# Products with u from PSUM, and all sums of v rows on TensorE, in the last two tiles of an expert layer

## The reference, cut to what matters

```
act = gelu(sum over d of h[t, d] * u[expert(t, head, k), d])
w   = gate(t, head, k) * act
out[t, :] += w * v[expert(t, head, k), :]      over 8 heads and 16 picks
```

## Time and profile before

| | |
|---|---|
| median of 3 runs | 3301.13 us (3296.62 to 3303.43) |
| profiled execution, span from first to last instruction | 3366.8 us |
| granted TensorE clock, mean of the span | 0.927 of full |
| busy share of the span: PE / DVE / POOL / ACT | 79% / 68% / 67% / 22% |
| moved by DMA | 1185.41 MB, mean 352 GB/s |

### The profile page before, as it was taken

The page is one execution under the profiler, slowest core; times in us unless marked ns, Lnnn a source line. Parts: engine busy times, 40 slices in busy tenths (PEclk is TensorE's granted clock), DMA queues, the critical chain, the costliest instruction groups (busy, mean ns, idle before and its releaser), DMA issues.

```text
span 3366.8 us, 25897 instructions
## 1 busy us (share of the span) xinstructions
PE 2658.0 (79%) x7200; PEld 1257.8 (37%) x7200; DVE 2274.4 (68%) x4952; ACT 737.2 (22%) x1644; POOL 2267.3 (67%) x2074
## 2 busy tenths in 40 slices
PE   7866778998888778987887868998888776666667
PEld 3444333444354333433344423334435332222222
DVE  1559964579579984668659994568758995455443
ACT  2411121223221121223221121223322111111111
POOL 0025677777766777777776677777776676777776
PEclk9888899999998899999999889999999898988989
DMA  5248999999999999999999899999999999999998
GB/s 185 75 172 301 345 345 408 406 405 368 361 388 351 379 341 400 407 407 362 350 396 381 325 361 384 405 406 393 358 389 368 335 328 350 346 370 371 368 362 332
DMA packets 351442, 1185.41 MB, mean 352 GB/s; under 512 B 37666, under 2 KB 38212, under 8 KB 351044
## 3 DMA queue, kind: packets, MB, share of 16 engines
q0 software_dynamic: 294912, 1073.87, 84.2%
q1 hardware_dynamic: 56388, 109.88, 8.9%
HBM read 1181.52 MB, written 2.10 MB: 352 GB/s over the span
## 4 chain that ended last, share of the span: by engine, by line
POOL 27%; PE 23%; DVE 20%; issue 17%; DMA 11%; another core or an unknown queue 1%; ACT 1%; DVEq 0%; POOLq 0%; ACTq 0%
POOL v_ring L468 13%; POOL u_ring L468 13%; PE peer_acc L1258 12%; DMA v_ring<-in_peer_v,experts 8%; PE act_bank L1045 5%; DVE u_ring L986 4%; DMA u_ring<-in_peer_u,experts 4%; PE dve_bank L1045 2%; DVE work L752 2%; DVE work L741 1%; DVE work L749 1%; DVE work L738 1%; DVE work L931 1%; DVE work L933 1%
## 5 line engine op out<-in xcount | busy, mean ns | idle before, releaser
L1258 PE MATMUL peer_acc<-v_ring,diag 128*128 128x512 f32 x3584 | 1805.4, 645 | 647.1 <-DMA v_ring<-in_peer_v,experts 296.7
L986 DVE SCALAR_TENSOR_TENSOR u_ring<-u_ring,h 128x1024 f32<-128x1024 f32 x1024 | 1255.2, 1226 | 841.2 <-DMA u_ring<-in_peer_u,experts 730.1
L468 POOL DMA_INDIRECT v_ring<-in_peer_v,experts x1024 | 1146.9, 1120 | 524.3 <-issue 259.6
L468 POOL DMA_INDIRECT u_ring<-in_peer_u,experts x1024 | 1114.9, 1089 | 561.2 <-issue 308.9
L1258 PEld LDWEIGHTS peer_acc<-v_ring,diag 128*128 128x128 f32 x3584 | 688.5, 203 | 1647.7 <-issue 1009.4
L669 ACT ACTIVATE diag<-ident,wts 128x128 f32<-128x128 f32 x896 | 325.8, 397 | 1180.5 <-PE peer_acc L1258 580.9
L1045 PE MATMUL act_bank<-w_ring,hT 128*128 128x512 f32 x768 | 346.4, 598 | 0.7 <-ACT hT L508 0.7
L1045 PEld LDWEIGHTS act_bank<-w_ring,hT 128*128 128x128 f32 x768 | 147.5, 193 | 187.0 <-issue 185.6
L996 DVE SCALAR_TENSOR_TENSOR xs<-v_ring,wts,xs 128x1024 f32<-128x1024 f32 x128 | 164.5, 1285 | 49.5 <-DMA v_ring<-in_peer_v,experts 40.0
L1132 PE MATMUL act_bank<-hT,w_ring 128*128 128x256 f32 x768 | 175.6, 384 | 0.0
L1132 PEld LDWEIGHTS act_bank<-hT,w_ring 128*128 128x128 f32 x768 | 148.6, 194 | 39.4 <-issue 20.9
(11 more groups left out here) (158 smaller groups left out, 1540.0 us busy)
## 6 DMA issues: line engine op xcount, KB each, us to landing
w_ring<-in_w_in SPq DMA_DIRECT2D x24, 2048.0 KB
w_ring<-in_peer_w_q SPq DMA_DIRECT2D x16, 2048.0 KB
w_ring<-in_w_out SPq DMA_DIRECT2D x8, 2048.0 KB
u_ring<-in_peer_u,experts POOLq DMA_INDIRECT x1024
v_ring<-in_peer_v,experts POOLq DMA_INDIRECT x1024
xs<-in_x SPq DMA_DIRECT2D x4, 512.0 KB, 7.2
keysT<-in_peer_sub_keys SPq DMA_DIRECT2D x2, 1024.0 KB
out<-xs SPq DMA_DIRECT2D x4, 512.0 KB
```

Source lines behind the costliest of these rows:

```text
L468: pool.indirect_dma_start(ring[:, n % depth, :], None, table, bass.IndirectOffsetOnAxis(ap=experts[:, tile % TILES, e:e + 1], axis=0),).th ...
L986: tell(nc.vector.scalar_tensor_tensor(out=row, in0=row, scalar=1.0, in1=h2[:, tile % TILES, :], op0=ALU.mult, op1=ALU.mult, accum_out=dots ...
L1258: ins = nc.tensor.matmul(peer_acc[:, j * 512:(j + 1) * 512], diag[:, (v_count(c, s) - 1) % DIAGS, :], v_ring[:, n % V_RING, j * 512:(j + 1 ...
```

## The change

In chunks 48 to 63 (tiles 6 and 7), and only there:

- `slot_u` reads `h` from PSUM. The three `dve_bank` become slices of one PSUM tensor `dve_banks`, and at the first slot of a tile DVE copies `h2` of the tile (128 x 1024) into its first two banks. The multiplication then has one input in SBUF (the u row) and one in PSUM. Its output stays in SBUF.
- `by_vector` is false, so that PE sums all 16 v rows of a chunk and DVE none. ACT makes 16 diagonal matrices per chunk instead of 14.
- The counts of `v_used` follow (`v_count`, `v_done`), and POOL's waits with them.

The number, size and order of the gathers don't change, nor does anything in chunks 0 to 47.

```diff
@@ -79,6 +79,7 @@
+    LAST_TILES = (LAYERS * HALVES - 1) * HALF
@@ -277,7 +278,9 @@
-        dve_bank = [ctx.enter_context(nc.psum_tensor(f"dve_bank{i}", [P, 512], F32)) for i in range(DVE_BANKS)]
+        dve_banks = ctx.enter_context(nc.psum_tensor("dve_banks", [P, DVE_BANKS * 512], F32))
+        dve_bank = [dve_banks[:, i * 512:(i + 1) * 512] for i in range(DVE_BANKS)]
+        h_last = dve_banks[:, 0:D]
@@ -326,14 +329,22 @@
-        def by_vector(s):
-
-            return s % V_EVERY == V_EVERY - 1
+        def by_vector(c, s):
+
+            return c // PH < LAST_TILES and s % V_EVERY == V_EVERY - 1
 
         def v_count(c, s):
 
-            mine = s // V_EVERY + 1
-            return c * V_DVE + mine if by_vector(s) else c * V_PE + s + 1 - s // V_EVERY
+            shared = min(c, LAST_TILES * PH)
+            if by_vector(c, s):
+                return c * V_DVE + s // V_EVERY + 1
+            before = s // V_EVERY if c // PH < LAST_TILES else 0
+            return shared * V_PE + (c - shared) * SLOTS + s + 1 - before
+
+        def v_done(tile):
+
+            chunks = (tile + 1) * PH
+            return v_count(chunks, 0) - 1
@@ -967,7 +978,7 @@
-                dve.wait_ge(v_used, (tile + 1) * PH * V_PE)
+                dve.wait_ge(v_used, v_done(tile))
@@ -981,14 +992,20 @@
             def slot_u(c, s):
                 tile, n = c // PH, c * SLOTS + s
+                h = h2[:, tile % TILES, :]
+                if tile >= LAST_TILES:
+                    if c % PH == 0 and s == 0:
+                        assert count.n["bank"] == FRONTS * DVE_GROUPS
+                        link(nc.vector.tensor_copy(h_last, h))
+                    h = h_last
                 dve.wait_ge(u_landed[n % U_RING], 16 * (n // U_RING + 1))
                 row = u_ring[:, n % U_RING, :]
                 tell(nc.vector.scalar_tensor_tensor(
-                    out=row, in0=row, scalar=1.0, in1=h2[:, tile % TILES, :],
+                    out=row, in0=row, scalar=1.0, in1=h,
                     op0=ALU.mult, op1=ALU.mult, accum_out=dots[:, c % 2, s:s + 1]), u_used, "u_used")
@@ -1244,12 +1261,12 @@
-                last = head == PH - 1 and v_count(c, s) == (c + 1) * V_PE
+                last = head == PH - 1 and v_count(c, s) == v_done(tile)
```

More of the change, by code:

```diff
@@ L488, in _ @@
                             old_c, old_s = divmod(n - V_RING, SLOTS)
-                            pool.wait_ge(v_added if by_vector(old_s) else v_used, v_count(old_c, old_s))
+                            pool.wait_ge(v_added if by_vector(old_c, old_s) else v_used, v_count(old_c, old_s))
                         gather(v_rows, v_ring, V_RING, v_landed, c, s)
@@ L663, in slot_v @@
                     act.wait_ge(wts_ready, c + 1)
-                if by_vector(s):
+                if by_vector(c, s):
                     return
@@ L986, in slot_u @@
                 tell(nc.vector.scalar_tensor_tensor(
-                    out=row, in0=row, scalar=1.0, in1=h2[:, tile % TILES, :],
+                    out=row, in0=row, scalar=1.0, in1=h,
                     op0=ALU.mult, op1=ALU.mult, accum_out=dots[:, c % 2, s:s + 1]), u_used, "u_used")
             def slot_v(c, s):
-                if not by_vector(s):
+                if not by_vector(c, s):
                     return
```

## The result

The kernel after takes 3277.48 us (median of 5 runs, 3274.28 to 3280.91) against 3301.13 us for the kernel before (now also 5 runs, 3287.47 to 3303.43). By the medians that is 24 us less. The ratio of the runs is 0.9943, with a 95% interval of 0.9928 to 0.9958, which is 19 us (14 to 24). 68 us were forecast, with 3213 to 3262 us as the range. The sign was right, the size was not.

What follows compares the result with a forecast made beforehand. POOL's gather issue was taken to bound chunks 52 to 63, DVE chunks 48 to 51. Terms -63.6 - 10.3 + 1.4 + 3.1 = -69.4 us on the 3366.8 us span, scaled to 68.0, gave 3233 us, range 3213 to 3262.

Steps and rivals of the forecast that it cites:

- The reading of the bound: Chunks 52 to 63: POOL issues all the time at 2.89 us per slot; once undisturbed, transfers bind at 2.56.
- Step 1: Chunks 52 to 63: with h from PSUM, gathers lose the stretch caused by u products, 54.1 us of POOL time.
- Step 2: Chunks 52 to 63: without DVE's v products, PE's gaps at slots 7 and 15 close; most of 27.4 us waits goes.
- Step 3: Chunks 52 to 63: 192 slots at the transfers' 2.56 us give 491.5 us against 555.1, so -63.6 us.
- Step 4: Chunks 48 to 51: DVE is the bound and loses 8 v products of 1.285 us, so -10.3 us.
- Steps 5 and 6: Chunks 48 to 63: two copies of h into PSUM cost +1.4 us; the u product's PSUM operand costs 0.
- Step 8: The end: the last chunk's v products run at PE's rate, 64 matmuls instead of 56, so +3.1 us.
- C: Chunks 52 to 63: transfers go faster than 410 GB/s and POOL's own pace binds; 3218 us, chance 0.12.
- F: Chunks 48 to 63: PE at its lower clock makes the kernel slower, +133 us, 3431 us; chance 0.04.
- E: Chunks 52 to 63: memory gives gathers alone no more than 362 GB/s, so no gain there; 3295 us, chance 0.04.
- B: Chunks 52 to 63: the gathers' stretch goes but POOL's waits at chunk starts stay; 3245 us, chance 0.18.
- D: Chunks 48 to 63: gathers stay stretched despite h in PSUM, only DVE's v products go; 3263 to 3290 us, chance 0.06.

Runs made afterwards that it cites:

- b1: The kernel before with no edit, run and profiled once more: 3297.64 us, ratio 1.0004, profiled span 3294.6 us.
- c1: Kernel before with all v rows on PE and gathers of half rows (2 KB) in chunks 48 to 63, h in SBUF: 3350.76 us, ratio 1.0162.
- c3: Kernel before with POOL pauses (two memsets of a dead buffer) at the first slot of chunks 52 to 63: 3346.18 us, ratio 1.0143.
- b2: Kernel after, but DVE keeps its v products in all chunks, so only h from PSUM is new: 3288.54 us, ratio 0.9968.
- d2: The kernel before with no edit, its third profile: 3290.16 us.
- b3: Kernel after, but h stays in SBUF, so only the v rows on PE are new: 3288.57 us, ratio 0.9963.
- d4: Kernel before with h from PSUM alone, plus POOL pauses (two memsets) at the first slot of chunks 52 to 63: 3303.59 us, ratio 1.0019.

## Why the prediction was wrong, step by step

**The reading of the bound: wrong, and this is the step that failed.** The prediction said that POOL is "issuing all the time, at 555.1 / 192 = 2.89 us per slot", and subtracted 2.56 from it. The 2.56 was right; the 2.89 held for one execution. In the other two profiles of the kernel before chunks 52 to 63 take 503 and 508 us, 2.62 and 2.65 us per slot, and in their last third 2.57. The same sum made with b1's profile is 508 - 492 = 16 us instead of 63.6. The 47 us between them are the 21 us of waits and the 26 us of stretch that only the first profile has. In all it would have been 16 + 8.9 - 3.1 = 22 us, where the two comparisons gave 24 and 19 by the medians, 19 and 15 by the ratios.

Two warnings stood in the rows. The span was 65.7 us above the median of the runs, with 6.8 us between the highest and the lowest of the three runs; the prediction scaled it away, or laid it on POOL's gathers at 0.032 us each, for 12 us. The right reading was that the 66 us might be the very waste that the change was to remove. And the earlier trace rows with the 411 GB/s of the earlier trace rows showed, inside the kernel before, a spell in which stretched gathers cost nothing: the products stood 2.56 us apart with h in SBUF. I used them for the rate of the transfers and didn't ask how long such spells last.

**Step 1, stretch of the gathers:** the mechanism is as described. It is gone after (939 and 938 ns), and c1 and c3 show its price where the transfers don't cover it. Its size in an ordinary execution was 28 us of POOL's time (200.8 + 187.2 - 383 x 0.94), not 54, and 13 of that lay under the transfers; from chunk 60 on all of it did.

**Step 2, gaps of PE:** PE's clock rose from 0.89 to 0.98 as foreseen, but b2 reaches 496 us at 0.87. The claim that the waits behind these gaps matter for chunks 52 to 63 falls: the wait of 3.63 us that the prediction read as one of them is one of the six that b1 and d2 don't have, though DVE takes slots 7 and 15 in both.

**Step 3, chunks 52 to 63 after the change:** 491.5 worked out, 492.2 and 492.0 measured.

**Step 4, chunks 48 to 51:** -8.9 with the copy, -8.7 measured (202.8 to 194.1). Alone, h gave 1.1 us (b2) and the v products 5.1 (b3); the other 2.5 us come only with both, or are the scatter of single profiles.

**Steps 5 and 6, copy and PSUM operand:** the product takes 1221 ns, and 1226 with both inputs in SBUF. The some 65 ns more that the prediction drew from the Trainium skill (VectorE: DVE Perf Modes, the section on the TRN2 errata) don't show in the instruction's duration. The second copy takes 1.23 us in d4 (at 2934), where 1.4 had been taken; what the copies cost in time was not measured by itself.

**Step 8, the end:** +3.1 foreseen, +6.2 measured (42.2 to 48.4). PE's part was nearly right (2.4 us more from the weights to the last addition, 26.8 to 29.2). What was missed is that with POOL ahead of the transfers the last gathers wait in a queue: the lag at the last product is 12.1 us instead of 6.9. Part of what chunks 52 to 63 gain by the gathers' starts is paid here.

**The rivals.** C and F did not come: the products stand 2.56 us apart, PE's clock is 0.98. E fell: 405 GB/s over 492 us of gathers alone. B fell with its waits: the stretch takes 492 us, not over 500. D's 3263 to 3290 holds the measured 3277, and that is chance: the gathers are released. The rival that was missing is that the transfers usually hide a good part of the stretch already, which is the plainest of rivals to a change that speeds up an issuer whose transfers are at 362 of 410 GB/s.

## What to carry to other kernels

When the profiled execution is longer than the runs by about as much as the change is to bring (here 65.7 and 68 us), first find out whether the surplus sits in the stage that the change is for; a second profile would have settled it here, and a list of the single long waits, with what the other engines did in them, would have raised the doubt. Where an issuer and the transfers are near to each other, divide a stage into chunks and look at its best ones: if the kernel already reaches the transfers' pace in some, the gain is only the share of chunks in which it doesn't. And what such a change buys may be steadiness more than time: the same disturbance cost the kernel before 47 us and the kernel after next to nothing.

## What the runs showed of the hardware

**A gather and a DVE instruction with two large SBUF inputs.** If the instruction is running when the gather starts, the gather ends 0.81 us after it. From chunk 52 to the end, over all 14 profiles, this holds within 0.02 us for 1399 of the 1414 gathers that started in such an instruction, 0.13 us or more before its end; the 15 others started in its first 0.1 us and took 0.94. If the gather started first, neither is longer: in 1156 such cases no gather took over 1.0 us and no product over 1.29. In the timeline of b1 above a product starts at 3226.99, inside a gather of 0.94, and takes its usual 1.22. The Trainium skill (SBUF — State Buffer, Who interferes with whom) says that a VectorE instruction with two SBUF inputs contends with a GpSimd instruction that reads SBUF, which these rows bear out for a gather that reads its indices there. It also says of the port they share that the second to issue waits for the first to finish. For the order product first this trace agrees; for the order gather first it doesn't, since the product is not held until the gather's end.

**The effect can fall in step with the transfers.** The stretch lengthens POOL's loop just to the transfers' pace and then stays, with the lag constant within 0.2 us over whole chunks (chunks 58, 62 and 63 of b1). Why it stays is argued and not tested by itself: a product that comes later stretches the gather more, which slows POOL until the transfers have caught up. Nothing in the kernel asks for this order, and a pause of 2 us is enough to leave it.

**Transfers from HBM.** Gathers of 4 KB rows ran at 405 GB/s over 492 us on one core. The Trainium skill (DMA: Bandwidth & Descriptors, Where 436 GB/s comes from) gives about 358 GB/s per core for transfers from HBM, as one of two equal shares of what a memory stack carries; with one core at work this was passed by 13%. What a second core at work would change, no run here shows.
